# The last 4096 modulation columns move from TensorE in the recurrent part to VectorE in the merge stage

## The reference, cut to what matters

```
mod_lat = silu(c) @ w_mod + b_mod            # 1024 x 6144, one vector
mod_ctx = silu(c_ctx) @ w_mod + b_mod
sh1, sc1, g1, sh2, sc2, g2 = split(mod_lat, 6)
hx = modulate(rms_norm(x), sh1, sc1)         # columns 0 to 2047
...
gdn_x = gated delta rule, chunk by chunk, both directions
y = sigmoid(g_a) * (attn @ w_pa) + sigmoid(g_d) * (gdn @ w_pd)      # merge
x = x + g1 * (y @ w_out)                     # columns 2048 to 3071
x = x + g2 * conv_ffn(modulate(rms_norm(x), sh2, sc2), ...)         # the rest
```

## Time and profile before

| | us |
|---|---|
| median of 3 runs (2566.88 to 2572.82) | 2572.14 |
| span of the profiled execution, first to last instruction | 2568.3 |
| PE busy in it | 2510.1 |
| DVE busy | 1372.8 |
| ACT busy | 1011.3 |

### The profile page before, as it was taken

How to read it: one execution, slowest core, us unless ns; L and a number is a source line. 1 busy time by engine, 2 the same in 40 slices (tenths; PEclk the granted TensorE clock), 3 DMA queues, 4 the chain that set the end, 5 groups by cost and what they waited for, 6 DMA issues and landing times.

```text
span 2568.3 us, 46219 instructions
## 1 busy us (share of the span) xinstructions
PE 2510.1 (98%) x19822; PEld 2049.1 (80%) x19822; DVE 1372.8 (53%) x1942; ACT 1011.3 (39%) x1666; POOL 257.3 (10%) x218
## 2 busy tenths in 40 slices
PE   7999999999999999999999999999999999999999
PEld 5766788778888888788888877788888876888887
DVE  4454898446667333566653555553453455552542
ACT  4354775333334223333333437332233356321232
POOL 0300002224321000111111010100001010100001
PEclk9999999989999999999999999999999999999999
DMA  7211210340006233222323221233223211322332
GB/s 282 91 60 58 74 58 26 110 141 20 4 4 236 90 99 131 81 94 97 99 90 99 90 75 50 90 99 97 93 98 99 91 58 58 99 94 95 99 99 74
DMA packets 70475, 231.30 MB, mean 90 GB/s; under 512 B 7808, under 2 KB 10240, under 8 KB 70144
## 3 DMA queue, kind: packets, MB, share of 16 engines
q1 hardware_dynamic: 69408, 226.52, 26.3%
q10 hardware_dynamic: 864, 1.84, 0.2%
HBM read 217.84 MB, written 10.49 MB: 89 GB/s over the span
## 4 chain that ended last, share of the span: by engine, by line
PE 91%; DVE 4%; ACT 2%; DMA 1%; issue 1%; POOL 0%; SPq 0%; POOLq 0%; DVEq 0%; ACTq 0%
PE ps L313 62%; PE ps L2774 6%; PE ps L1735 4%; PE ps L323 3%; PE ps L803 2%; PE ps L1777 1%; PE ps L1760 1%; PE ps L1741 1%; PE ps L792 1%; PE ps L2828 1%; PE ps L2859 1%; PE ps L1933 1%; PE ps L2037 1%; DVE row_max L833 1%; PE ps L818 1%
## 5 line engine op out<-in xcount | busy, mean ns | idle before, releaser
L294 DVE TENSOR_TENSOR w_lo<-ring,w_hi 128x1024 fp32r<-128x1024 f32 (+1 forms) x339 | 416.8, 1230 | 814.8 <-ACT w_hi L286 814.5
L286 ACT CAST w_hi<-ring 128x1024 fp32r<-128x1024 f32 (+1 forms) x339 | 354.1, 1044 | 907.4 <-PE ps L313 808.9
L313 PE MATMUL ps<-u_hi,w_hi 128*128 128x512 f32 x864 | 338.4, 392 | 2.5 <-DVE u_lo L2584 2.5
L313 PE MATMUL ps<-u_hi,w_lo 128*128 128x512 f32 x864 | 337.1, 390 | 0.0
L313 PE MATMUL ps<-u_lo,w_hi 128*128 128x512 f32 x864 | 337.1, 390 | 0.0
L313 PE MATMUL ps<-mid_hi,w_hi 128*128 128x512 f32 x672 | 261.4, 389 | 0.0
L313 PE MATMUL ps<-mid_lo,w_hi 128*128 128x512 f32 x672 | 261.4, 389 | 0.0
L313 PE MATMUL ps<-mid_hi,w_lo 128*128 128x512 f32 x672 | 261.4, 389 | 0.0
L313 PEld LDWEIGHTS ps<-u_hi,w_hi 128*128 128x128 f32 x864 | 162.7, 188 | 38.1 <-issue 3.2
L313 PEld LDWEIGHTS ps<-u_lo,w_hi 128*128 128x128 f32 x864 | 162.9, 189 | 33.9 <-issue 0.5
L313 PEld LDWEIGHTS ps<-u_hi,w_lo 128*128 128x128 f32 x864 | 162.7, 188 | 34.0
(11 more groups left out here) (498 smaller groups left out, 4610.0 us busy)
## 6 DMA issues: line engine op xcount, KB each, us to landing
ring<-in_w_up SPq DMA_DIRECT2D x44, 512.0 KB, 3.6
ring<-in_w_in SPq DMA_DIRECT2D x42, 512.0 KB, 3.7
ring<-in_w_merge SPq DMA_DIRECT2D x32, 512.0 KB, 3.6
ring<-in_w_mlp1a SPq DMA_DIRECT2D x32, 512.0 KB, 3.6
ring<-in_w_mlp2a SPq DMA_DIRECT2D x32, 512.0 KB, 3.6
ring<-in_w_mlp1b SPq DMA_DIRECT2D x32, 512.0 KB, 3.6
ring<-in_w_mlp2b SPq DMA_DIRECT2D x32, 512.0 KB, 3.7
ring<-in_w_gdn_in SPq DMA_DIRECT2D x24, 512.0 KB, 3.6
```

What stands on the lines that cost most here:

```text
L286: nc.scalar.copy(w_hi[:, slot, 0:width], ring[:, n % RING, 0:width]).then_inc(*hi_ok.one())
L294: nc.vector.tensor_tensor(w_lo[:, slot, 0:width], ring[:, n % RING, 0:width], as_f32(w_hi[:, slot, 0:width]), ALU.subtract).then_inc(*lo_o ...
L313: mm = nc.tensor.matmul(dst[:, a:b], w[wi][:, k * P:(k + 1) * P], src[xi][:, k0 + k, a:b], start=start and k == wi == xi == 0, stop=stop a ...
```

## The change

The 16 pieces leave the recurrent part: their loads, matmuls, row copies, column matmuls and biases, and the waits that guarded them. ACT makes silu(c) once more as 8 plain columns (`c_columns`) in the first stage. In the merge stage the same 16.8 MB are loaded as 32 tiles of 128 rows x 1024 columns of `w_mod` (four pieces of 1 KB for each partition), into four slots. For each 1024 columns, DVE multiplies the tile of 128 rows k by silu(c) of these rows and adds it to a running sum (`rest_step`: one tensor_scalar, then seven scalar_tensor_tensor, 128x1024), and PE then sums over the 128 partitions with 8 matmuls that have `rest_sum` as stationary operand and one column of ones as the moving one. DVE adds the bias. The values for the context are no longer made, since none of these columns is used for it.

```
-                for i in range(2 * N_REST):            # stage_gdn, SP
-                    ...
-                    sp.dma_start(rest_home(i), rest[i]).then_inc(*rest_landed(i)[0].dma())
...
+            def rest_of_step(i):
+                return range(min(max(5 * i // 4, 0), len(rest)), min(max(5 * (i + 1) // 4, 0), len(rest)))
...
+                        def rest_loads(i):             # stage_merge, SP, called behind each unit's load
+                            for j in rest_of_step(i - RING):
+                                if j >= REST_SLOTS:
+                                    sp.wait_ge(*rest_added.at(j - REST_SLOTS + 1))
...
+                                sp.dma_start(rest_w[:, j % REST_SLOTS, :].rearrange("p (g c) -> p g c", g=4),
+                                             rest[j]).then_inc(*rest_in[j % REST_SLOTS].dma())
+                        stream_weights(sp, 4 * KD, beside=rest_loads)
...
+                            for c in rest_chunks_after(n):         # PE, behind products 4, 7, 11, 14
+                                pe.wait_ge(*rest_added.at((c + 1) * KD))
+                                for m in range(KD):
+                                    mm = nc.tensor.matmul(ps[:, 7, c * KD + m:c * KD + m + 1],
+                                                          rest_sum[:, c % 2, m * P:(m + 1) * P], ones[:, 0:1],
...
                         for n in range(2 * KD):        # DVE
                             split_lo(dve, 2 * n + 2)
+                            rest_step(2 * n - 2)
                             dve.wait_ge(*gate_ok.at(n + 1))
                             split_lo(dve, 2 * n + 3)
+                            rest_step(2 * n - 1)
+                            for c in rest_chunks_after(n - 1):
+                                rest_bias(c)
```

More of the change, by code:

```diff
@@ L52 @@
 MOD_FIRST = 16
+REST_SLOTS = 4
+REST_SUMS_AFTER = (4, 7, 11, 14)
 BUFFERS = 8
@@ L268, in stream_weights @@
                 sp.dma_start(ring[:, n % RING, 0:w.shape[1]], w).then_inc(loaded[n % RING], 16)
+                if beside is not None:
+                    beside(n - at["issued"])
             at["issued"] = last
@@ L425, in _ @@
                                              ACT.Silu).then_inc(*silu_c.one())
+                    nc.scalar.activation(c_columns[:], vec("c", 0, 16).rearrange("p (k v) -> p k v", v=2)[:, :, 0],
+                                         ACT.Silu).then_inc(*silu_c.one())
                     for j, k in enumerate(arrival):
@@ L2280, in _ @@
                                     LAT).then_inc(*unit_used.one())
+                            for c in rest_chunks_after(n):
[3 more added lines that the diff above has]
+                                                          rest_sum[:, c % 2, m * P:(m + 1) * P], ones[:, 0:1],
+                                                          start=True, stop=True)
+                                mm.then_inc(*rest_summed.one())
                     @block.scalar
@@ L2298, in _, with rest_step, rest_bias @@
                     def _(dve):
+                        def rest_step(i):
+                            for j in rest_of_step(i):
+                                k, acc = j % KD, rest_sum[:, j // KD % 2, :]
+                                w = rest_w[:, j % REST_SLOTS, :]
+                                dve.wait_ge(*rest_in[j % REST_SLOTS].at(16 * (j // REST_SLOTS + 1)))
+                                if k == 0:
+                                    if j >= 2 * KD:
+                                        dve.wait_ge(*rest_summed.at(j // KD - 1))
+                                    else:
+                                        dve.wait_ge(*sig("gdn_lo").at(0))
+                                    nc.vector.tensor_scalar(acc, w, c_columns[:, 0:1], None, ALU.mult).then_inc(*rest_added.one())
+                                else:
+                                    dve.wait_ge(*rest_added.at(j))
+                                    nc.vector.scalar_tensor_tensor(out=acc, in0=w, scalar=c_columns[:, k:k + 1], in1=acc,
+                                                                   op0=ALU.mult, op1=ALU.add).then_inc(*rest_added.one())
+                        def rest_bias(c):
+                            m = MOD_FIRST + c * KD
+                            dve.wait_ge(*rest_summed.at(c + 1))
+                            nc.vector.scalar_tensor_tensor(out=mod[:, m:m + KD, 0], in0=ps[:, 7, c * KD:(c + 1) * KD],
+                                                           scalar=1.0 if m == 4 * KD else 0.0, in1=vec("b_mod", m, KD),
+                                                           op0=ALU.add, op1=ALU.add).then_inc(*mod_b.one())
                         split_lo(dve, 1)
@@ L2320, in on_vector @@
             def on_vector(dve):
+                dve.wait_ge(*sig("mod_b").at(0))
                 dve.wait_ge(*unit_used.at(0))
```

114 lines of the change are left out of this document (12 added, 102 removed).

## The result

| | before | after |
|---|---|---|
| median of the runs shown with the result | 2571.28 us (2566.88 to 2572.82) | 2633.2 us (2626.08 to 2646.18) |
| ratio, 95% interval | | 1.024 (1.0217 to 1.0262) |
| span of the profiled execution | 2568.3 us | 2632.0 us |
| granted clock, mean | 0.992 | 0.978 |

The account below looks back on a forecast made before the run. PE was taken to bound the kernel before, and a DVE loop waiting for tiles to bind the merge stage after. 2568.3 - 24 + 69 + 5 = 2618 us span, plus 3.8: 2622 us median, range 2594 to 2655.

Parts of the forecast that it names:

- The mechanism: Merge stage: DVE waits a whole DMA each step, so its 8.2 us loop binds over PE's 5.45 us unit; chance 0.70.
- case 4: Merge stage: tiles are there when DVE asks and PE never waits, giving 2556 us; chance 0.05.
- Rival 3: Merge stage: tiles land late, from small pieces or three loads in a row; 9.7 us loop, 2661 us; chance 0.09.
- The 4.4 us: Merge stage: estimate from first issue to both landings, from 2.0 us fixed and 436 GB/s, against 4.9 us by the rows.
- the recurrent gain: Recurrent part: 24 us gained by removing the 16 pieces, bounds 17 to 32 us.
- removal of 27 us: Recurrent part: silu(c) matmuls 16.3 us, column matmuls 8.6, copies and biases about 1.5, load wait 0.75; together 27 us.
- the 3 us given back: Recurrent part: estimate for PE waiting for DVE where it did modulation work before, 3 us off the gain.
- 74 us forecast: Merge stage: loss of 69 us from the DVE loop over 26 steps plus 5 us for the clock.
- the column sums then fall into PE's idle time and cost nothing: Merge stage: PE's 32 column sums are free under the longer DVE loop; 8.4 us in full otherwise.
- The clock term of 5 us: Merge stage: 5 us added for longer stretches of PE at half clock, bounds 0 and 70 us.
- Rival 2: Merge stage: PE's clock stays low for most of it, units up to 10.9 us, up to 2690 us; chance 0.12.
- the 3.8 us from span to median: Whole kernel: the median was taken to lie 3.8 us above the span.

Follow-up runs that it names:

- run 2: Changed kernel with each weight tile requested two steps ahead, all work the same: 2556.63 us, ratio 0.9939.
- run 7: Changed kernel with each weight tile requested one step ahead, nothing left out: 2556.12 us, ratio 0.9955.
- run 4: Changed kernel with the tile issued ahead of the ring load within each step: 2605.18 us, ratio 1.0135.
- run 1: Changed kernel without the added tile loads, sums and column sums, modulation columns 2048 to 6143 set to bias alone: 2550.02 us, ratio 0.9929.
- run 3: Changed kernel with the first two groups of column sums behind products 5 and 8 instead of 4 and 7: 2620.71 us, ratio 1.0192.
- run 10: Changed kernel with tiles requested two steps ahead and 80 unused matmuls at the first 10 of 16 old recurrent places: 2553.26 us, ratio 0.9943.
- run 6: Changed kernel with columns 2048 to 6143 set to bias alone, plus 16 unused matmuls at the first two old recurrent places: 2552.75 us, ratio 0.9928.
- run 8: Changed kernel with tiles requested two steps ahead and 16 unused matmuls at the first two old recurrent places: 2564.54 us, ratio 0.9965.
- Run 5: Changed kernel with columns 2048 to 6143 set to bias alone, plus 128 unused matmuls at all 16 old recurrent places: 2551.22 us, ratio 0.992.
- run 9: Changed kernel with tiles requested two steps ahead and 128 unused matmuls at all 16 old recurrent places: 2557.14 us, ratio 0.9946.

## Why the prediction was right, and where its sizes were off

**The mechanism was right.** The steps of a DVE loop with a whole DMA in it are there row for row: landing 4.62 us in the step shown and 4.6 in the median (forecast 4.5), sum 1.28 (1.29), first product 0.75 (0.8), issue 0.33 and 0.04 (the same), DVE idle for 4.9 to 5.8 us ahead of nearly every first sum (4 to 5). Runs 2 and 7 show that the wait is the cause and not the added work: the same instructions with the request one or two steps earlier lose nearly nothing beyond PE's time for the column sums. The rival of the opposite sign was worth its number: case 4, tiles there when DVE asks, was put at 2556 us, and run 2, which makes just that true, gave 2556.63. That it agrees within 1 us is in part luck: case 4 has 15.6 us below the kernel before, run 2 has 13.8 below that of its session. One sign was off: PE was to be busy about two thirds of the merge stage and was busy for 0.78 of it, since at half clock the same work takes longer.

**Rival 3, late tiles, fell.** Second of two, a tile landed 4.6 us after its issue in pieces of 1 KB, a ring unit in pieces of 4 KB 4.7 us in run 4; first of two they took 3.9 and 3.6 us. So the small pieces cost 0.3 us at most, not 1.5. From the first issue to both landings it is 0.33 + 0.04 + 4.62 = 5.0 us here (forecast 4.9). The 4.4 us that the prediction worked out from the Trainium skill (DMA: Bandwidth & Descriptors, Anatomy of one DMA), an estimate, were too few; the page gives its fit for loads that GpSimd issues, and these are issued by SP.

**The term that was mis-sized most is the recurrent gain: 24 us forecast, 14.6 in the profiled execution.** The 14.6 lies outside the bounds of 17 to 32 us; the whole stayed in range because the range was wider. The prediction's removal of 27 us holds. If each microsecond at half clock costs half of one, the marks at full clock are 801.3 - 8.5 = 792.8 us before, 786.7 - 20.5 = 766.2 after, and 766.7 in run 1: 26.1 to 26.6 us. That this reckoning is sound is borne out by runs 2, 3, 4 and 7, where it gives 765.5 to 767 us, and by run 10, where ten of the 16 places should come to 766.5 + 15.4 x 10 / 16 = 776.1 and the mark is 776.3; in runs 6 and 8 it comes out 2 to 4 us too high, which stays unexplained.

Run 5 splits the removal: at 782.1 with no half-clock time, the matmuls with silu(c) are 782.1 - 766.7 = 15.4 us (term 16.3), and the column matmuls, copies and load wait 792.8 - 782.1 = 10.7 us (terms 8.6 + 1.5 + 0.75).

What was wrong is the 3 us given back. They were for PE waiting for DVE in place of the modulation work, and that hardly came: from 485 to 580 us PE waits 2.1 us for DVE after and 1.3 before, and 6.6 and 6.1 us in all. What took the gain is the clock. The prediction had "17 us if the stops without a name and the low clock grow with the thinner work" as its lower bound; the low clock grew more. Half-clock time went from 17 to 41 us, 12 us of the gain, though the new stops of PE are few and short: 2.42 us for ACT's `gdn_kd`, which the old matmuls had covered, is the longest seen. Part of it is the execution: with the same code in this part, runs 2, 3, 4 and 7 have the mark at 778.9 to 781.8 us, a gain of 19.5 to 22.4 us, with 24 to 31 us at half clock.

Run 5 shows the cause of the rest: the work put back costs 1.2 us of the median (3.4 by the marks) instead of 16, because it holds the clock. In the profile of the changed kernel this reads as a full PE row of 25.00 us with 493 records at 0.50. One window must not be compared alone, though: run 2, without any filler, has 852 records and a clock of 1.00 in the same 25 us, and its half-clock time lies ahead of them. Over the whole stretch from 485 to 580 us the clock was 0.78 in the changed kernel, 0.84 to 0.87 in runs 1, 2, 3, 4 and 7, and 1.00 in runs 5, 9 and 10.

**The merge stage: 74 us forecast (69 + 5 for the clock), 79.1 measured.** The loop is (79.1 + 2.8) / 26 = 3.15 us longer than PE's unit, 8.6 us against 8.2, and 8.6 by the low parts in the timeline. The step that failed is "the column sums then fall into PE's idle time and cost nothing". Their work does; their wait doesn't. PE's program has the sums behind a given unit, and when DVE is behind, PE stands before them (20.0 us, longest 10.7) while the next unit's parts are ready. It comes out of this late, and at the lower clock (0.84 and 0.88 in the windows around 900 us), and then DVE waits for it. In run 3, where this wait is 0.4 us, the loss is 71.0 us, a loop of (71.0 + 2.8) / 26 + 5.45 = 8.3 us: the prediction's 8.2 to within 0.1. So 8.1 us of the 79.1 are this wait and what follows from it; 5.9 of them can be seen as DVE's waits at 912.28 and 966.38.

**The clock term of 5 us** stood in the wrong place. Mean clock in the merge stage was 0.88, 53 us at half clock. Run 3 still had 0.92 there, some 35 us at half clock, and its loss of 71.0 us is what the loop alone gives (69), so these 35 us cost some 2 us at most: PE took them from its idle time, as the prediction argued. The other half-clock time can be no more than a part of the 8.1 us. Its real price lay in the recurrent part. Rival 2 (up to 2690 us) did not come.

**Without idle time the column sums cost 7.4 us** in runs 2 and 7, forecast 8.4.

By the profiled executions: 24 - 14.6 = 9.4 us less gain, 79.1 - 74 = 5.1 more loss, 0.8 less behind the merge: 13.7 us. The spans are 2632.0 measured and 2618 forecast. The medians are only 11.2 us apart, because the 3.8 us from span to median were too many: the median here lies 1.2 us above the profiled span.

## What to carry to other kernels

Work that fits an engine's idle time can still stop it, if its operand is requested behind the instruction that it follows: look in the order of the queue for what must have happened before the request, and sum up that loop before summing up work. Here one number, the look-ahead, turned +2.4% into -0.6%, and four slots were already there for it. And work taken from TensorE in a stretch of small dependent matmuls may be worth far less than its busy time, if the granted clock there falls with it: compare the clock over the whole stretch and in several executions, not only the chain.

## What was not expected of the hardware

The granted clock follows what TensorE does in a way that busy time doesn't show: in the recurrent part of the changed kernel it was 0.50 from 540 to 565 us with PE busy in every microsecond. From 485 to 580 us it was 0.78, and 1.00 when 128 more matmuls of 128x256 were strewn in (runs 5 and 9). How long a stretch stays at the lower level also differs from execution to execution of one kernel: with no filler or with little of it, executions mostly lay 7 to 20 us apart (the changed kernel, runs 1, 2, 4, 6, 7, 8), though the four of run 3 lay within 2.4 us; with all of it they lay 1.1 and 4.2 us apart. The kernel before, with the old matmuls, lies between: 6 to 12 us in four sessions. What sets it is left open.

The second of two 512 KB loads lands 0.8 to 1.0 us later than the first whichever it is (3.9 and 4.7 us in run 4, 3.6 and 4.6 in the changed kernel).
